# Making one layer's memory values in the last but one expert bunch instead of in that layer

## The reference, cut to what matters

```python
mkv = rms_norm_2(mem, mem_norm[l]) @ w_mem_kv[l]      # 256 x 1024 @ 1024 x 512
mk, mv = jnp.split(mkv, 2, axis=-1)                   # keys and values, 256 x 256 each
sm = einsum('bhsd,bhmd->bhsm', mq, mk) * HEAD_DIM ** -0.5
om = einsum('bhsm,bhmd->bhsd', softmax(sm), mv)       # four heads of 64
```

## Time and profile before

| | us |
|---|---|
| three runs of the kernel | 707.16, 707.76 (median), 708.52 |
| the profiled execution, its own time | 706.99 |
| its span, first to last instruction | 705.2 |
| PE busy | 637.2 (90%) |
| DVE busy | 355.0 |
| ACT busy | 331.6 |
| mean granted clock of TensorE, as a share of full speed | 0.986 |

### The profile page before, as it was taken

The page is one execution under the profiler, slowest core; times in us unless marked ns, Lnnn a source line. Parts: engine busy times, 40 slices in busy tenths (PEclk is TensorE's granted clock), DMA queues, the critical chain, the costliest instruction groups (busy, mean ns, idle before and its releaser), DMA issues.

```text
span 705.2 us, 12717 instructions
## 1 busy us (share of the span) xinstructions
PE 637.2 (90%) x5093; PEld 507.6 (72%) x5094; DVE 355.0 (50%) x820; ACT 331.6 (47%) x782; POOL 46.0 (7%) x57
## 2 busy tenths in 40 slices
PE   6999999999999999777586899999989999999996
PEld 4977899779854555534353589878878898888886
DVE  1543666654830131101010448889775577897743
ACT  3455656542120132112120344779875546888842
POOL 6001000000000000000000233010000020100000
PEclk9999999999999999998899999999999999999999
DMA  9994335496989999999999948017533071093101
GB/s 291 326 324 152 120 120 177 139 340 265 412 348 381 414 423 420 419 421 421 421 420 416 311 132 276 12 45 255 179 121 121 1 240 60 1 299 123 58 1 60
DMA packets 74110, 166.86 MB, mean 237 GB/s; under 512 B 3391, under 2 KB 58465, under 8 KB 62785
## 3 DMA queue, kind: packets, MB, share of 16 engines
q1 hardware_dynamic: 71920, 160.87, 61.8%
q0 software_dynamic: 2000, 5.06, 2.1%
q10 hardware_dynamic: 128, 0.08, 0.0%
HBM read 164.92 MB, written 1.07 MB: 235 GB/s over the span
## 4 chain that ended last, share of the span: by engine, by line
PE 66%; DVE 10%; DMA 9%; ACT 6%; SPq 6%; issue 2%; DVEq 0%; ACTq 0%
PE psum L942 11%; PE psum L944 10%; PE psum L943 10%; SPq L809 6%; DMA probs_values<-in_w_expert_up_dram 4%; PE psum L997 4%; PE psum L1374 4%; DMA ring<-in_w_expert_down_dram 4%; PE psum L1324 3%; PE psum L1388 3%; PE psum L1259 3%; PE psum L1306 2%; DVE w_low L2420 2%; PE psum L1351 2%; PE psum L1089 1%
## 5 line engine op out<-in xcount | busy, mean ns | idle before, releaser
L942 PE MATMUL psum<-a_high,w_high 128*128 128x256 f32 x512 | 149.4, 292 | 4.5 <-ACT tiles L1623 1.7
L943 PE MATMUL psum<-x_low,w_high 128*128 128x256 f32 x512 | 144.7, 283 | 0.0
L944 PE MATMUL psum<-a_high,w_low 128*128 128x256 f32 x512 | 144.6, 282 | 0.0
L2420 DVE TENSOR_TENSOR w_low<-ring,w_high 128x1024 fp32r<-128x1024 f32 (+1 forms) x73 | 100.9, 1395 | 29.5 <-ACT w_high L1734 29.5
L942 PEld LDWEIGHTS psum<-a_high,w_high 128*128 128x128 f32 x512 | 97.8, 191 | 14.7 <-issue 7.2
L1734 ACT ACTIVATE w_high<-ring 128x1024 fp32r<-128x1024 f32 (+1 forms) x79 | 96.2, 1222 | 10.6 <-DMA ring<-in_w_in_dram 7.2
L943 PEld LDWEIGHTS psum<-x_low,w_high 128*128 128x128 f32 x512 | 97.9, 191 | 0.1
L944 PEld LDWEIGHTS psum<-a_high,w_low 128*128 128x128 f32 x512 | 97.9, 191 | 0.0
L1374 PE MATMUL psum<-ring,q_c 128*32 128x256 f32 x544 | 51.9, 411 | 22.7 <-DMA probs_values<-in_w_expert_up_dram 6.3
L942 PE MATMUL psum<-w_high,a_high 128*128 128x256 f32 x240 | 69.5, 290 | 1.8 <-DVE mix_low L2431 1.5
L2342 DVE TENSOR_TENSOR tiles<-tiles,psum 128x256 f32<-128x256 f32 x8 | 3.4, 422 | 122.8 <-ACT tiles L1790 122.7
(11 more groups left out here) (357 smaller groups left out, 1234.2 us busy)
## 6 DMA issues: line engine op xcount, KB each, us to landing
ring<-in_w_in_dram SPq DMA_DIRECT2D x36, 1024.0 KB, 8.2
ring<-in_w_expert_down_dram SPq DMA_DIRECT2D x24, 1024.0 KB, 20.8
ring<-in_w_expert_gate_dram SPq DMA_DIRECT2D x20, 1024.0 KB, 18.2
ring<-in_w_expert_up_dram SPq DMA_DIRECT2D x14, 1024.0 KB, 24.7
ring<-in_w_out_dram SPq DMA_DIRECT2D x12, 1024.0 KB, 5.0
ring<-in_w_mem_kv_dram SPq DMA_DIRECT2D x4, 1024.0 KB, 12.6
probs_values<-in_w_expert_down_dram SPq DMA_DIRECT2D x3, 1024.0 KB, 17.7
ring<-in_w_expert_gate_dram SPq DMA_DIRECT2D x4, 512.0 KB, 6.6
```

What stands on the lines that cost most here:

```text
L942: pe.matmul(dst, left[0], right[0], start=first, stop=False)
L943: pe.matmul(dst, left[0], right[1], start=False, stop=False)
L944: return pe.matmul(dst, left[1], right[0], start=False, stop=last)
L2420: dve.tensor_tensor(w_l, raw_of(n), as_f32(w_h), ALU.subtract).then_inc(lows, 1)
```

## The change

The load of layer 1's `w_mem_kv` value half leaves the ring of the second block. It is put into SP's queue behind the loads of bunch 6's items and ahead of bunch 7's, into slot 11, which no later item uses. Both products are made by PE behind bunch 6's `add_back`, into the two halves of bank 4, and PE then waits until ACT has copied the bank into a buffer of its own, `last_mem_v`. The jump over `more_rounds` comes behind that. The two `mv` jobs of layer 1 are gone from the order of jobs, and so are their two copies on ACT and the wait for them ahead of the M heads' outputs. The other items of layer 1 keep their slots, but `out1_0` to `out1_3` are loaded one place earlier.

```diff
-    ITEMS += ([f"mem_k{_l}", f"mem_v{_l}"] + _in if _l == 0 else [f"mem_k{_l}"] + _in + [f"mem_v{_l}"])
+    ITEMS += ([f"mem_k{_l}", f"mem_v{_l}"] if _l == 0 else [f"mem_k{_l}"]) + _in
...
+LAST_MEM_V_SLOT = 11
...
-        if l:
-            for tt in range(2):
-                behind[13 + tt].append(("mv", l, tt))
...
+        last_mem_v = sb("last_mem_v", [P, 2 * COLS])
...
-        mem_v = v_nat[:, 1024:2048].rearrange("p (l t n) -> p l t n", l=LAYERS, t=2)
+        mem_v = [a.rearrange("p (t n) -> p t n", t=2) for a in (v_nat[:, 1024:1536], last_mem_v[:, :])]
...
+            def last_user(k):
+                return max(m for m in range(FIRST_EXPERT, FIRST2) if slot_of(m) == k)
...
+            sp.wait_ge(*expert_done(last_user(LAST_MEM_V_SLOT)))
+            sp.dma_start(slots[:, LAST_MEM_V_SLOT], source("mem_v1")).then_inc(last_mem_v_in, 16)
...
             with sp.If(some):
+                sp.wait_ge(last_mem_v_ready, 1)
...
                 else:
-                    from_act(("mv", l, 1))
+                    if l == 0:
+                        from_act(("mv", l, 1))
...
+            def last_memory_values():
+
+                pe.wait_ge(last_mem_v_in, 16)
+                for tt in range(2):
+                    mm = natural(bank(4)[:, COLS * tt:COLS * tt + COLS], memT[1], tt, slots[:, LAST_MEM_V_SLOT], 0, COLS)
+                mm.then_inc(last_mem_v_ready, 1)
+                pe.wait_ge(last_mem_v_out, 1)
...
                     if b == BUNCHES - 2:
                         pe.wait_ge(memT_out, KC // 2)
+                        last_memory_values()
                         more_rounds(some)
...
                     if b == BUNCHES - 2:
+                        act.wait_ge(last_mem_v_ready, 1)
+                        act.activation(last_mem_v[:, :], bank(4), ACT.Copy).then_inc(last_mem_v_out, 1)
                         more_rounds()
```

More of the change, by code:

```diff
@@ L677, in build @@
         gu_half = sem("gu_half")
+        last_mem_v_in, last_mem_v_ready, last_mem_v_out = (sem("last_mem_v_in"), sem("last_mem_v_ready"),
+                                                           sem("last_mem_v_out"))
         gu_ready, gate_exped, hidden_done = sem("gu_ready"), sem("gate_exped"), sem("hidden_done")
@@ L764, in expert_done @@
                 return (gu_ready, b + 1) if j < GATE_UP else (y_ready, 2 * b + 2)
+            def last_user(k):
+                return max(m for m in range(FIRST_EXPERT, FIRST2) if slot_of(m) == k)
             def last_expert_use(k):
-                return expert_done(max(m for m in range(FIRST_EXPERT, FIRST2) if slot_of(m) == k))
+                return expert_done(last_user(k))
             def free_for_experts(n):
@@ L1292, in values @@
                         return [v2[:, tt, 3, HD * (h // 3):HD * (h // 3) + HD] for tt in range(2)]
-                    return [mem_v[:, l, tt, HD * h:HD * h + HD] for tt in range(2)]
+                    return [mem_v[l][:, tt, HD * h:HD * h + HD] for tt in range(2)]
                 for m in range(T_JOBS[kind]):
@@ L1613, in take @@
                     l, tt = job[1:]
-                    op = act.activation(mem_v[:, l, tt, :], src[:, 0:256], ACT.Copy)
+                    op = act.activation(mem_v[l][:, tt, :], src[:, 0:256], ACT.Copy)
                 elif kind == "tile2":
```

## The result

The kernel after takes 711.28 us (median of 8 runs, 709.15 to 711.91) against 708.28 for the kernel before beside it (8 runs, 707.16 to 710.34): ratio 1.0036, 95% interval 1.0021 to 1.0051. It was timed twice more, 1.0029 (1.0011 to 1.0048) and 1.0026 (1.0013 to 1.0038). By these ratios it is slower, by 1.8 to 2.5 us; the medians of the three pairs differ by 3.0, 1.4 and 1.8 us. 707.6 was forecast, with a range of 705.8 to 711.2, set on a median of 707.76 for the kernel before, which came out at 708.28 here. The profiled execution took 711.51 us, its span is 709.7.

A forecast was written before the change was run, and what follows sets the result against it. Loads were taken to end the experts' stage, with PE close behind, and PE's order to set layer 1's M heads. PE's longer chain, +4.1, and the M heads, -4.3, gave -0.2 on 707.76: 707.6 us, range 705.8 to 711.2.

The forecast's parts named there:

- the loads don't end bunch 7, PE does: Bunch 7: PE ready for the down products at 395.3 us, behind the loads at 393.67; rival, loads end it, 0.20.
- its 2.49 us: Loads ahead of bunch 7: one more 1.049 MB item at 421 GB/s makes the last matrix 2.49 us later.
- D: Time from the start of bunch 6's add_back to the start of bunch 7's down products, forecast at 395.3 us.
- The gap of 3.65 us behind the jump: PE's stop after 27 of 64 gate records, read as waiting for code; forecast to go; staying was a rival, 0.20.
- 4.93 was taken: Bunch 7's gate half: the clock falls in the wait before it, so it takes 4.93 us instead of 3.6.
- The M stretch: Layer 1's M heads, first head's output product to the last one's: forecast to fall from 16.79 to 12.50 us.
- the jump at 4.68 us: PE's jump behind the new products and ACT's copy: takes 4.68 us, from 377.0 to 381.7, with PE empty.
- The sum: PE's chain through bunch 7: first gate product 381.9, plus 4.93 and 3.6 us, then 4.9 us: ready at 395.3.
- The third rival: Jump waits 1.1 us longer, up to 2, or less returns in layer 1; net +1.4 to +2.4 us; chance 0.10.
- three signs named for being wrong: Jump below 3 us, an "issue" gap in bunch 7's up half, or layer 1's M stretch above 13.5 us.
- The gain in layer 1, 4.29: Layer 1's M heads: removing 7.10 us of jobs brings up 2.81 us of waiting, so 4.29 us are saved.
- E: Second block: time from the start of bunch 7's add_back to the end of PE's last product; no forecast size.

The follow-up runs named there:

- before again: The kernel before, profiled and timed once more with no edit; ratio 1.0007 (0.9991 to 1.0023).
- one in each layer: Kernel before with one of the two products moved to layer 0's M heads, the other kept in layer 1's, experts untouched; ratio 0.9974 to before.
- fewer fillers before: Kernel before with 8 instead of 12 unread filler products in the first block's wait for the router; ratio 0.9987 to before.
- the third after: The kernel after, profiled and timed a third time with no edit; ratio 1.0026 (1.0013 to 1.0038) to before.
- no jump: Kernel after without the block of extra rounds on PE, so PE has no jump there; ratio 0.9980 to before.
- jobs out: Kernel before without layer 1's two mv jobs and their item, nothing in their place; layer 1 reads layer 0's memory values; ratio 0.9960 to before.
- fewer fillers, after: Kernel after with 8 instead of 12 unread filler products in the first block's wait for the router; ratio 1.0018 to before.
- products behind the jump: Kernel after with both new products, and PE's wait for ACT's copy, moved behind PE's jump; ratio 0.9992 to before.

## Why the prediction was wrong

**Right.** In the kernel after the loads don't end bunch 7, PE does. The new load is hidden (30.95 without it against 30.88 to 31.05), so its 2.49 us are not tested there; by itself it added 1.8 to 2.8 us to D. The products take 7.07 us, ACT's copy 0.60. The gap of 3.65 us behind the jump in the earlier trace rows is gone: 64 gate records without a stop. The clock fell to 0.50 behind the wait (5.16 us for the gate half; 4.93 was taken). The M stretch takes 12.49.

**The step that failed: the jump at 4.68 us.** It took 6.14 us, with 6.07 and 6.12 in the other two profiles. That is 1.4 to 1.5 us on a chain where nothing covers it. The sum had D at 395.3 - 365.5 = 29.8; it is 30.9 to 31.05, 1.1 to 1.25 us more, since PE reached the jump some 0.2 us earlier than reckoned; the gate and up halves took what the sum gave them (8.55 us against 8.53). The path was right, this term was too small: the transfer that the jump waits for starts 3.6 us into it, where it started 2.2 us into it in the row that I read. The low one was one record of one execution, taken as the price. The third rival had a longer jump, by 1.1 us up to 2, but from a transfer already under way for the new products. That isn't what happened: in the kernel after the transfer ahead of it starts at 372.4, 7.5 us before the jump, and takes 1.1 us, and kernels without the new products have 5.92 to 6.00 as well (before again, one in each layer, fewer fillers before). Its sum was off too: 1.1 to 2 us on -0.2 are +0.9 to +1.8, not +1.4 to +2.4, unless half a microsecond less comes back in layer 1, which it names but doesn't price. And of the three signs named for being wrong none came: a jump that is too long was not among them.

**The gain in layer 1, 4.29.** It is 3.8 to 4.0 by E, since up to 0.5 us goes back behind the stretch (22.03 against 21.50 us). The stretch was cut at the last head's output product, and what is queued behind it was taken as unchanged.

**The total.** D of before is 25.68 and 26.67, so the experts lose 4.2 to 5.4 us, in the mean 4.8; with 3.9 given back that is +0.9 (+1.4 for the first profile of each). With the three other profiles whose experts are those of before (25.00, 25.46, 25.88) the mean loss is 5.2 and the sum +1.3. The timings have +1.8 to +2.5. The profiles have the missing 1.1 us upstream, from bunch 3's first down product to bunch 6's: 85.9 and 85.6 us in the two of before, 86.5 to 87.3 in the three of after. Here from PE's timeline of before and of the third after:

```profile
275.08 0.62 PE L1388 MATMUL psum<-ring,tiles 128*32 128x512 f32 x1 [0.51 <-ACT tiles L1795]
...
360.96 3.64 PE L1388 MATMUL psum<-ring,tiles 128*32 128x512 f32 x32 [0.58 <-ACT tiles L1795]
```

```profile
275.96 0.62 PE L1395 MATMUL psum<-ring,tiles 128*32 128x512 f32 x1 [0.51 <-ACT tiles L1811]
...
362.74 3.64 PE L1395 MATMUL psum<-ring,tiles 128*32 128x512 f32 x32 [0.50 <-ACT tiles L1811]
```

But two kernels with before's experts have 86.8 and 87.0 there (one in each layer, fewer fillers before), and one with the new products has 85.5 (no jump). So it isn't shown to belong to the change, and it stays open. Why the transfer of code starts ahead of the jump in some kernels and inside it in others stays open too: PE's work ahead of it is the same in jobs out and in before.

The Trainium skill, Runtime: NRT & Kernel Launch, section Instruction fetch mechanics, says that crossing from one block of code to the next is mostly hidden, and that a taken branch out of the window waits. The runs agree with the second where the jump took 4.7 to 6.1 us, each time until 2.5 us behind the start of a transfer; the 0.47 us of jobs out, with the same work ahead of its jump, show that the code can also be there. To the first they show exceptions, both shortly behind the jump and at full DMA load: straight code waited 4.83 us (fewer fillers, after) and 3.65 us. In the profile of before that is the one stop of PE over 1 us that is put down to "issue", with 43 transfers in all.

## What to carry to other kernels

Before work is put ahead of a jump, look at what hid the jump: here it ran beside `add_back`, and the one new wait in front of it put all of its 6 us on PE's chain. Ask of each wait what is queued behind it, and put it behind the jump where the result isn't needed before; here this took the loss away, but the loads kept it from being a gain. A duration that decides a sum wants more than one profile, and a product taken out of a softmax's wait gives back only part of its time.

## What was not expected of the hardware

- One instruction, in one program, took 4.68 us in one execution and 5.97 in another; over the study it took 0.46, 4.7 or 5.9 to 6.1 us. Where it took 0.46 us in the kernel after with fewer fillers, PE stopped for 4.83 us two matmul records on. ACT's and DVE's own jumps over the same block took 0.05 and 0.07 us in the kernel before.
- After a 3.83 us wait for a load the granted clock stayed at 0.50 and 0.58 for 6.5 us (products behind the jump); after the 7.1 us wait in the kernel after it was 0.50 for 2.6 us. In the kernel after the clock had fallen well inside the wait already (0.74 over the wait, 0.89 over the shorter one), so less of the low stretch was left for the work.
- The items behind the new one were issued slowly. From SP's timeline (start, us to issue), the four gate items in the kernel before, then the new item and what follows it in the kernel after:

```profile
337.37 7.64 SPq L809 DMA_DIRECT2D ring<-in_w_expert_gate_dram  x4
```

```profile
338.01 2.15 SPq L842 DMA_DIRECT2D ring<-in_w_mem_kv_dram  x1
341.23 19.19 SPq L813 DMA_DIRECT2D ring<-in_w_expert_gate_dram  x4
360.47 0.43 SPq L813 DMA_DIRECT2D mixT<-in_w_expert_up_dram  x1
```

The DMA engines stayed busy meanwhile. No run prices this by itself; in the kernel after it is hidden behind PE's chain together with the load.
